# A two-block fp32 transformer kernel: the first product taken for both row tiles in turn, its loads in smaller pieces, the convolution ahead of one split

## The reference

```python
def causal_depthwise_conv3(u, w):
    s = u.shape[1]
    up = jnp.pad(u, ((0, 0), (CONV_W - 1, 0), (0, 0)))
    return up[:, 0:s] * w[0] + up[:, 1:s + 1] * w[1] + up[:, 2:s + 2] * w[2]

def short_conv_mixer(h, w_in, conv_w, w_out):
    bcx = h @ w_in
    b_gate, c_gate, u = jnp.split(bcx, 3, axis=-1)
    y = b_gate * causal_depthwise_conv3(c_gate * u, conv_w)
    return y @ w_out

mix = short_conv_mixer(rmsnorm(h, a_pre_norm[l]), a_w_in[l], a_conv_w[l], a_w_out[l])
h = h + rmsnorm(mix, a_post_norm[l])
```

## Time and profile before

| what | value |
| --- | --- |
| median of 3 runs | 1029.12 us (1028.97 to 1029.18) |
| the profiled execution | 1029.98 us |
| its span, first to last instruction | 1028.2 us |
| mean granted TensorE clock of the span | 0.998 |
| PE busy | 1020.1 us, 99% |
| DVE, ACT, POOL busy | 67%, 55%, 13% |
| data moved | 203.56 MB, mean 198 GB/s |

### The profile page before, as it was taken

The page is one execution under the profiler, slowest core; times in us unless marked ns, Lnnn a source line. Parts: engine busy times, 40 slices in busy tenths (PEclk is TensorE's granted clock), DMA queues, the critical chain, the costliest instruction groups (busy, mean ns, idle before and its releaser), DMA issues.

```text
span 1028.2 us, 14332 instructions
## 1 busy us (share of the span) xinstructions
PE 1020.1 (99%) x4783; PEld 839.0 (82%) x4783; DVE 684.2 (67%) x1034; ACT 567.0 (55%) x925; POOL 137.1 (13%) x219
## 2 busy tenths in 40 slices
PE   9999999999999999999999999999999999999997
PEld 6999888888877778888888888888887688888886
DVE  5777856656788985656668565656787685655643
ACT  5665654545567864444556454454676854454542
POOL 1100450000143152000014000000400220000002
PEclk9999999999999999999999999999999999999999
DMA  9575577566643467667576775757643355757551
GB/s 364 174 238 187 184 226 242 179 226 200 211 145 126 146 225 249 217 196 243 178 235 210 233 222 188 245 176 243 207 168 122 98 171 176 239 184 238 187 175 46
DMA packets 104174, 203.56 MB, mean 198 GB/s; under 512 B 52976, under 2 KB 57472, under 8 KB 104128
## 3 DMA queue, kind: packets, MB, share of 16 engines
q1 hardware_dynamic: 101952, 197.44, 59.0%
q0 software_dynamic: 1888, 5.17, 1.8%
q10 hardware_dynamic: 288, 0.37, 0.1%
HBM read 187.20 MB, written 1.05 MB: 183 GB/s over the span
## 4 chain that ended last, share of the span: by engine, by line
PE 96%; DVE 1%; ACT 1%; DMA 0%; POOL 0%; issue 0%; POOLq 0%; DVEq 0%; SPq 0%; ACTq 0%
PE pG L2108 16%; PE pG L2116 16%; PE pG L2112 16%; PE pD L2108 11%; PE pD L2112 11%; PE pD L2116 11%; PE pG L2097 2%; PE pG L2101 2%; PE pG L2098 2%; PE pT L2125 1%; PE pD L2142 1%; PE pD L2101 1%; PE pD L2097 1%; PE pD L2098 1%; PE pG L2422 1%; PE pG L2125 1%
## 5 line engine op out<-in xcount | busy, mean ns | idle before, releaser
L1693 DVE TENSOR_TENSOR w_low<-raw,w_high 128x1024 fp32r<-128x1024 f32 x340 | 410.3, 1225 | 195.8 <-ACT w_high L1370 185.7
L1370 ACT ACTIVATE w_high<-raw 128x1024 fp32r<-128x1024 f32 x340 | 354.7, 1056 | 207.0 <-PE pG L2116 135.9
L2108 PE MATMUL pG<-w_high,xTh 128*128 128x512 f32 x712 | 220.0, 390 | 0.0
L2112 PE MATMUL pG<-w_high,xTl 128*128 128x512 f32 x712 | 219.6, 389 | 0.0
L2116 PE MATMUL pG<-w_low,xTh 128*128 128x512 f32 x712 | 219.4, 390 | 0.2 <-DVE w_low L1693 0.2
L2116 PEld LDWEIGHTS pG<-w_low,xTh 128*128 128x128 f32 x712 | 133.6, 188 | 28.2 <-DVE w_low L1693 0.6
L2112 PEld LDWEIGHTS pG<-w_high,xTl 128*128 128x128 f32 x712 | 133.6, 188 | 28.1 <-DVE xTl L1739 0.2
L2108 PEld LDWEIGHTS pG<-w_high,xTh 128*128 128x128 f32 x712 | 133.3, 188 | 27.3
L1484 ACT ACTIVATE gate<-pG,stat 128x256 f32<-128x256 f32 x102 | 48.4, 474 | 140.1 <-PE pG L2116 124.0
L2108 PE MATMUL pD<-w_high,aTh 128*128 128x512 f32 x348 | 107.8, 391 | 0.0
L2116 PE MATMUL pD<-w_low,aTh 128*128 128x512 f32 x348 | 107.5, 390 | 0.0
(11 more groups left out here) (312 smaller groups left out, 1112.9 us busy)
## 6 DMA issues: line engine op xcount, KB each, us to landing
raw<-in_stream SPq DMA_DIRECT2D x340, 512.0 KB, 4.6
aF<-aB SPq DMA_DIRECT2D x320, 32.0 KB, 2.6
post<-in_posts POOLq DMA_DIRECT2D x5, 512.0 KB, 4.7
early<-in_stream SPq DMA_DIRECT2D x4, 512.0 KB, 13.1
xF<-hg SPq DMA_DIRECT2D x32, 64.0 KB, 2.5
xF<-hg POOLq DMA_DIRECT2D x32, 64.0 KB, 2.3
first_w<-in_stream SPq DMA_DIRECT2D x3, 512.0 KB, 5.8
h<-in_x SPq DMA_DIRECT2D x2, 512.0 KB, 11.9
```

Source lines behind the costliest of these rows:

```text
L1370: sc.activation(w_high[:, slot(static):slot(static) + CHUNK], raw_of(static), ACT.Copy).then_inc(w_high_done, 1)
L1693: ve.tensor_tensor(w_low[:, slot(static):slot(static) + CHUNK], raw_of(static), w_high[:, slot(static):slot(static) + CHUNK].bitcast(F32), ...
L2108: pe.matmul(dst, ah, w_high[:, where:where + n], start=start, stop=False)
L2112: pe.matmul(dst, al, w_high[:, where:where + n], start=False, stop=False)
```

## The change

`first` takes the two tiles in turn for each group of 128 features, so that each piece of `first_w` serves both at once. `first_w` is loaded in six pieces of 512 columns and the quarters and halves of `xt` go between them. DVE's `opening` makes four products of 256 columns and then two of 512, in place of `turn` for phase 0. ACT loads only the 91 columns of gains and taps; the identity follows on SP's queue behind `raw` 0, and PE waits for it behind `first`. Two of the 11 matmuls on zeros go. The turning of tile 0's block 0 moves one group later in block 1's product. ACT's `high` of chunks 3, 4 and 5 moves behind the next step of the convolution (or gate). Some semaphores are merged (`halo_and_logs`, `proj_done0`, `end_weights`), with waits for the same events.

```diff
-TURN_IN_PRODUCT = (2, 2)
+TURN_IN_PRODUCT = (3, 2)
-WARM_UPS = 11
+WARM_UPS = 9
+PIECE = 512
...
 def walk_first_block(step):
-    step("turn", 0, 0)
-    step("first", 0)
+    step("opening", 0)
     step("parts", 0, 0)
-    step("turn", 1, 0)
-    step("first", 1)
+    step("opening", 1)
+    step("first",)
     split(step, 0)
     step("norm", 0)
     split(step, 1)
     step("G", 0, 0, 0)
     split(step, 2)
-    step("high", 3)
     step("T", 0, 0, 0)
-    step("low", 3)
-    step("high", 4)
+    split(step, 3)
     step("Y", 0, 0, 0)
-    step("low", 4)
-    step("high", 5)
+    split(step, 4)
...
 def walk_second_block(step):
     step("G", 0, 1, 0)
-    step("low", 5)
+    split(step, 5)
     split(step, 6)
...
-                sp.dma_start(xt[0][:, 0:512], x_turned[0, :, 0:512]).then_inc(xt_left, 16)
+                left_quarter, second_quarter, right_half = slice(0, 256), slice(256, 512), slice(512, D)
+                load_x(0, left_quarter, xt_first)
                 first_weights(0)
+                load_x(1, left_quarter, xt1_loaded)
                 first_weights(1)
-                sp.dma_start(xt[0][:, 512:D], x_turned[0, :, 512:D]).then_inc(xt_right, 16)
+                load_x(0, second_quarter, xt_second)
+                load_x(1, second_quarter, xt_second)
                 first_weights(2)
-                sp.dma_start(xt[1][:], x_turned[1]).then_inc(xt1_loaded, 16)
+                load_x(0, right_half, xt_right)
+                load_x(1, right_half, xt_right)
+                for i in (3, 4, 5):
+                    first_weights(i)
                 load_raw(0)
+                sp.dma_start(consts[:, C_ID:C_FEATS], consts_in[:, C_ID:C_FEATS]).then_inc(ident_loaded, 16)
                 load_h(0)
...
-                sc.dma_start(consts[:, 0:C_ROPE], consts_in[:, 0:C_ROPE]).then_inc(ident_loaded, 16)
+                sc.dma_start(consts[:, C_FEATS:C_ROPE], consts_in[:, C_FEATS:C_ROPE]).then_inc(xt_first, 16)
...
+            def opening(half, ph):
+                if half == 0:
+                    ve.wait_ge(xt_first, 32)
+                    gained_quarter(0, 0).then_inc(warm_ready, 1)
+                    ve.wait_ge(xt1_loaded, 16)
+                    gained_quarter(1, 0).then_inc(warm_ready, 1)
+                    ve.wait_ge(xt_second, 32)
+                    for t in range(2):
+                        gained_quarter(t, 1).then_inc(hg_ready[t], 1)
+                else:
+                    ve.wait_ge(xt_right, 32)
+                    for t in range(2):
+                        gained(t, GAIN[0], 1, xt[t][:, 512:D])
...
+            def first(ph):
+
+                for kt in range(KT):
+                    for i in range((kt * MIX.cols + PIECE - 1) // PIECE, ((kt + 1) * MIX.cols - 1) // PIECE + 1):
+                        pe.wait_ge(first_loaded[i], 16)
+                    for t in range(2):
+                        if kt == 0:
+                            pe.wait_ge(warm_ready, t + 2)
+                        elif kt in (2, 4):
+                            pe.wait_ge(hg_ready[t], kt // 2)
+                        mm = pe.matmul(gate_bank(MIX, t, 0)[:, 0:MIX.cols], hg[t][:, kt * P:(kt + 1) * P],
+                                       first_w[:, kt * MIX.cols:(kt + 1) * MIX.cols], start=kt == 0, stop=kt == KT - 1)
+                        if kt == KT - 1:
+                            mm.then_inc(first_done1 if t else g_done0, 1)
                 pe.wait_ge(ident_loaded, 16)
```

More of the change, by code:

```diff
@@ L911, in build @@
         w_freed = sem("w_freed")
-        first_loaded = [sem(f"first_loaded{i}") for i in range(FIRST)]
+        first_loaded = [sem(f"first_loaded{i}") for i in range(FIRST * CHUNK // PIECE)]
         first_done1, warm_ready = sem("first_done1"), sem("warm_ready")
         h_loaded = rows2("h_loaded")
-        xt_left, xt_right, xt1_loaded = sem("xt_left"), sem("xt_right"), sem("xt1_loaded")
+        xt_first, xt_second, xt_right, xt1_loaded = sem("xt_first"), sem("xt_second"), sem("xt_right"), sem("xt1_loaded")
         ident_loaded, tables_loaded = sem("ident_loaded"), sem("tables_loaded")
@@ L1035, in moved_block, with x_count @@
             return network(ph) * (ph.nb - 1) + b + t + shift * (RING // (ph.cg + ph.kd))
+        def x_count(i):
+            return 3 + i + (1 if i < 3 else 2)
         def branch_done(eng, t, k, half):
@@ L1083, in first_weights, with load_x @@
                 def first_weights(i):
-                    sp.dma_start(first_w[:, i * CHUNK:(i + 1) * CHUNK], stream[i]).then_inc(first_loaded[i], 16)
+                    cols = slice(i * PIECE, (i + 1) * PIECE)
+                    sp.dma_start(first_w[:, cols], stream[i * PIECE // CHUNK][:, i * PIECE % CHUNK:i * PIECE % CHUNK + PIECE]).then_inc(first_loaded[i], 16)
+                def load_x(t, cols, loaded):
+                    sp.dma_start(xt[t][:, cols], x_turned[t, :, cols]).then_inc(loaded, 16)
                 def load_raw(c):
@@ L1337, in finish @@
                     pool.wait_ge(h_ready[0], 2 * FFN4.index + half + 1)
[L1338 removed]
+                    weighted(0, slice(512 * half, 512 * half + 512)).then_inc(end_weights, 1)
                 pool.wait_ge(end_m, 1)
[L1340 to L1342 removed]
+                pool.tensor_tensor(rr[0], ms[0], half_neg[:, 0:1], ALU.pow).then_inc(end_weights, 1)
+                pool.wait_ge(end_weights, 3)
                 pool.tensor_scalar(hg[0][:, 0:512], hg[0][:, 0:512], rr[0], None, ALU.mult).then_inc(out_by_pool, 1)
                 pool.wait_ge(end_m, 2)
[L1345 removed]
+                pool.tensor_tensor(rr[1], ms[1], half_neg[:, 0:1], ALU.pow).then_inc(end_weights, 1)
             steps = {f.__name__: f for f in (start, parts, squares, rest, norm, right, second_low, spread, reload, finish, tail, rope, S, LAT, VC, decay, GNvar)}
@@ L1711, in low, with gained_quarter @@
                 split_low(c, c)
+            def gained_quarter(t, quarter):
+                cols = slice(256 * quarter, 256 * quarter + 256)
+                g = feats[:, 2 * quarter:2 * quarter + 2].unsqueeze(2).broadcast_to([P, 2, P])
+                return ve.tensor_tensor(hg[t][:, cols].rearrange("p (k r) -> p k r", k=2), xt[t][:, cols].rearrange("p (k r) -> p k r", k=2),
+                                        g, ALU.mult)
             def gained(t, col, half, src):
@@ L1745, in turn @@
                     sinks()
-                if p == 0:
-                    for half in range(2):
-                        ve.wait_ge(xt1_loaded if t else (xt_left, xt_right)[half], 16)
-                        gained(t, GAIN[p], half, xt[t][:, 512 * half:512 * half + 512])
-                elif (t, p) not in RIGHT_ONLY:
+                if (t, p) not in RIGHT_ONLY:
                     for half in range(2):
                         gained_half(t, p, GAIN[p], half)
+            def opening(half, ph):
[11 more added lines that the diff above has]
+                        gained(t, GAIN[0], 1, xt[t][:, 512:D])
             def left(t, ph):
@@ L2084, in RL @@
                                  xTh[t][:, 4:8, :].rearrange("p k r -> p (k r)").bitcast(F32), ALU.subtract).then_inc(catT_ready[t], 1)
-            steps = dict(start=start, low=low, R=refill, left=left, turn=turn, parts=parts, second=second, second_low=second_low, spread=spread, gain=gain, rest=rest, finish=finish, tail=tail, join=join, G=G, V=V, T=T, Y=Y,
+            steps = dict(start=start, low=low, R=refill, opening=opening, left=left, turn=turn, parts=parts, second=second, second_low=second_low, spread=spread, gain=gain, rest=rest, finish=finish, tail=tail, join=join, G=G, V=V, T=T, Y=Y,
                          rope=rope, QKT=QKT, S=S, N=N, AT=AT, LAT=LAT, KPE=KPE, U=U, RROPE=RROPE, RSUM=RSUM, MT=MT, MS=MS, MN=MN, VC=VC, RT=RT, RM=RM, GNvar=GNvar, GNout=GNout,
@@ L2131, in start @@
                     pe.matmul(pD[1][:, 0:512], warm[:, 0:P], warm[:], start=True, stop=True)
-                pe.wait_ge(ident_loaded, 16)
-            def first(t, ph):
-                for kt in range(KT):
-                    if kt % 4 == 0:
-                        pe.wait_ge(hg_ready[t], kt // 4 + 1)
-                    if t == 0:
-                        for i in range((kt * MIX.cols + CHUNK - 1) // CHUNK, ((kt + 1) * MIX.cols - 1) // CHUNK + 1):
-                            pe.wait_ge(first_loaded[i], 16)
-                    mm = pe.matmul(gate_bank(MIX, t, 0)[:, 0:MIX.cols], hg[t][:, kt * P:(kt + 1) * P],
-                                   first_w[:, kt * MIX.cols:(kt + 1) * MIX.cols], start=kt == 0, stop=kt == KT - 1)
-                mm.then_inc(first_done1 if t else g_done0, 1)
+            def first(ph):
[11 more added lines that the diff above has]
+                            mm.then_inc(first_done1 if t else g_done0, 1)
+                pe.wait_ge(ident_loaded, 16)
             def turn(t, p, ph):
```

44 lines of the change are left out of this document (18 added, 26 removed).

## The result

| | before | after |
|---|---|---|
| median of the runs, us | 1029.07 (1028.93 to 1029.46, 12 runs) | 1031.4 (1030.86 to 1031.96, 12 runs) |
| ratio, 95% interval | | 1.0022 [1.0015, 1.003] |
| profiled execution, us (span) | 1029.98 (1028.2) | 1031.96 (1030.1) |

The change makes the kernel slower by 2.3 us; I had forecast no change, 1029.1, with 1028.3 to 1029.8 as the range. The profiled execution of before, 1029.98, lies above all twelve runs of its kernel, and 1031.96 is the highest of the twelve after. Keep this in mind wherever a time from one profile stands beside a median. The page of the profile says little: PE is busy for the same 1020.1 us as in the earlier trace rows, in a span that is 1.9 us longer.

A forecast was written before the change was run, and what follows sets the result against it. PE bounds the kernel (busy 1020.1 of 1028.2 us), ACT and DVE its opening's end. First product 0.5 us earlier, turning +0.52, ACT's order +0.07, loads 0: sum +0.1, 1030.1 profiled, median 1029.1; range 1028.3 to 1029.8.

The forecast's parts named there:

- What bounds the kernel: Opening: PE bounds up to 18.5 us, ACT and DVE up to 23.16; the gain is how much earlier that turning comes.
- The first product's start: `first` on PE: starts at 5.35 us, not before 5.20 nor after 6.32, since 0.45 MB less must land first.
- rivals 2: Opening: the whole start is gained, ACT and DVE not being the bound; 1.1 us, 1028.0, chance 0.05.
- 4: Start of `first`: small loads start no sooner, so it begins at 6.2 and the time is 1029.7; chance 0.11.
- The other pieces have room: Loads during `first`: second quarters land at 6.7, right halves at 8.6 us; needed at 8.8 and 11.4.
- DMA and SP: Loads up to `h`: 12 issued in place of 6, same bytes; priced at 0, bounds 0 and +0.3 us.
- The turning and ACT's order: Block 1's product to second turning: turning behind nine passes costs 0.52 us, ACT's later splits 0.07.
- The clock's rise (1): `first` on PE: clock already up when it begins, second turning about 22.45; 0.7 us less, 1028.4, chance 0.20.
- The slower case (3): `first` on PE: idle gap delays the clock's rise, 0.5 us per us; worst 1038.7; chance 0.06, half beyond 0.2%.
- 0.04 for slower: Whole kernel: chance given to a slower result, beside 0.94 same and 0.02 faster; about 0.2%, 2.1 us, can be told.

The follow-up runs named there:

- experiment 4: The changed kernel with the constants loaded as before (109.5 KB in one load, none for the identity): 1031.17 us, ratio 1.0018.
- experiment 5: The kernel before with two extra 512 KB loads ahead of `raw` 0, the squares waiting for them too: 1031.78 us, ratio 1.0025.
- 14: The kernel before with short constants, DVE's split of chunk 3 ahead of block 0's taps and 10 matmuls on zeros: 1029.44 us, ratio 1.0002.
- Experiment 6: The kernel before with only the changed order: turning behind nine passes, ACT's splits 3 to 5 behind the taps: 1030.03 us, ratio 1.0007.
- experiment 15: The kernel before once more, unchanged and profiled anew: 1029.23 us, ratio 1.0001.
- Experiment 8: The kernel before with 5 matmuls on zeros in place of 11: 1031.25 us, ratio 1.0019.
- experiments 1: The changed kernel with coarse loads again, `first_w` in three of 512 KB and `xt` in four of 256 KB: 1032.92 us, ratio 1.0027.
- 2: The kernel before with only the changed kernel's fine loads of `first_w` and `xt`, first product in the old order: 1033.98 us, ratio 1.0046.
- experiment 9: The changed kernel with coarse loads of `first_w` and `xt` and 15 matmuls on zeros in place of 9: 1030.81 us, ratio 1.0016.
- 11: The kernel before with `first_w` in six loads of 256 KB, in runs of 1024 bytes: 1031.03 us, ratio 1.0021.
- experiments 10: The kernel before with `first_w` in six loads of 256 KB, rows of 2048 bytes: 1029.61 us, ratio 1.0004.
- experiment 12: The kernel before with `first_w` in three loads of 512 KB, two of them with runs of 2048 bytes: 1031.4 us, ratio 1.0021.
- 13: The kernel before with `first_w` in four loads of 384 KB, in runs of 1024 bytes: 1035.92 us, ratio 1.0064.
- experiment 3: The kernel before with each load of `xt` and `first_w` cut in two by partitions, 64 rows each: 1033.44 us, ratio 1.0041.

## Why the prediction was wrong

**What bounds the kernel: right.** "What the change is worth is therefore how much earlier the turning at 23.16 comes", it says. In all 18 profiles the time of the profiled execution is its turning and 1006.5 to 1006.8 us, with turnings from 22.48 to 29.00, so the two go together within 0.4 us. What I missed is that 23.16 was the turning of an execution 0.9 us above its median. Against it the medians look off: order +0.2 in the turning and +0.7 in the median, late landings +1.9 and +2.5, and turnings of 22.5 to 22.8 that bring no gain. Against the 22.6 of a median execution, an estimate, they fit to 0.1 or 0.2 us.

**The first product's start: close, and worth nothing.** (So rivals 2 and 4, a gain of the whole start and no earlier start, are both out.) 5.35 forecast, 5.00 measured, below my lower bound of 5.20 (the record of the last matmul on zeros runs to 5.21 and overlaps it; I had taken an end for a start).

**"The other pieces have room": wrong.** At 410 GB/s I had the second quarters at 6.7 and the right halves at 8.6. At 243 GB/s the second quarters were there only at 7.6 and the right halves at 11.1, and the pieces of `first_w` came late too. PE waited for them inside the product, which ended at 17.71 in the prediction's way of counting, not at 16.75: the whole of the earlier start was given back, and 0.47 us more.

**DMA and SP: the step that failed.** The prediction says: "Even if the small pieces made the chunks land 0.5 late, the splits 1 and 2 [...] have 0.5 us of room against the taps [...]. I price it at 0 (bounds 0 and +0.3)." The chunks landed 2.4 late and `h` 2.6, five times the allowance. The room was mis-sized as well. In the four profiles whose chain goes through the squares of `h` (the change, experiments 4, 5 and 14) the turning comes 9.38 or 9.39 us behind their start. Before it came 9.88 behind, so 0.5 us of room was there in that one execution; with a turning at 22.6 (the estimate above) there is next to none. So in the medians nearly all of the delay shows: `h` 2.4 later gave 2.5 us in experiment 5, and 1.85 later gave 1.8 in experiment 4; in the change it's 2.3 for the 2.6 read in the highest of its runs. A term priced at 0 was worth the whole loss. The reasoning that broke was "the bytes up to `h` are the same": it carried the rate of the earlier trace rows, measured on loads of 256 and 512 KB, over to loads of 128 and 256 KB. That left the term without an honest bound. No row of before had twelve small loads in flight; what it had, 266 GB/s up to 6.20, I read as the time to get going only, and as a bound for a start-up that lasts 5 us longer it would have given about (413 - 266)/413 of 5 us, 1.8 us more. SP's own issues, 12 in place of 6, put the issue of `h` from 4.46 to 8.33; I priced the queue's order and not its time.

**The turning and ACT's order: right.** Experiment 6 gives 1.86 and 4.69 where I had 1.84 and 4.67. In the change itself the same order is behind later inputs. In the timeline it's 3.34 from the start of block 1's product to `cv`, where 1.78 before and 0.52 for three passes make 2.30; the other 1.04 is the wait for split 1. I had looked at the operands of the turning and not at those of the three passes put ahead of it. From `cv` to the turning it's 4.68. That the old order loses as much when `h` is late (experiment 5, by way of ACT) shows that this new dependence adds little.

**The rivals.** The clock's rise (1) didn't matter to the change, since the first product isn't on the chain; that it moves from run to run is seen in experiment 15, where the eleven matmuls on zeros take 4.24 us in place of 4.87. The slower case (3) had the right sign and the wrong mechanism. Experiment 8 shows its price, close to what I had: a rise 3 us later, behind a gap of 2.6 us, costs 1.55 us in the turning. I had no rival in which the loads get slower, and 0.04 for slower was far too little: with one term unmeasured on both sides, the slow side should have held more.

## What to carry to other kernels

When a load that PE waits for is cut into pieces, count what stands behind it in the queue: here the start came 1.3 us earlier and what stood behind the pieces 2.4 to 2.6 us later. A transfer rate read from large loads isn't a bound for small ones; ask for a row with loads of that size, and where there is none, price the slow side too. A profile is of one execution: see first where its time lies among the runs, since here a baseline that was 0.5 us late passed for room and hid that `h` was already due. And a wait of 2.4 to 3.2 us ahead of the first product cost the clock's lower level on top of itself in experiments 1, 2 and 8; matmuls on zeros up to the landing gave it back (2.1 us between the medians, in experiment 9).

## What the runs showed of the hardware

- Loads of HBM rows into 128 partitions, between 4 and 9 us: 413 GB/s with six loads, 359 with nine (2048-byte rows of `first_w`), 284 with nine (runs of 1024 bytes), 243 to 270 with twelve; about 410 again from 9 us on, when the queue holds large loads. The DMA share was 0.82 in the change, 0.90, 0.92 and 0.94 in experiments 4, 11 and 2, but 1.02 and more in experiments 10, 12 and 13, so a full share isn't a full rate.
- Loads into 64 partitions (experiment 3): 243 GB/s at a share of 0.99 from 4 to 9 us and 235 at 1.05 from 9 to 14, with rows of 4096 and 2048 bytes.
- SP's issues of loads took 0.40 to 0.43 us each for the first ten loads of the change, 0.51 for the eleventh, and 0.63 to 0.80 for the next four.
- The granted clock's column can say 1.00 where the pace of the matmuls is half (experiments 1 and 8); the count of matmuls in a stretch is the surer reading. A wait of 1.8 us inside the product, behind matmuls at the upper level, cost nothing of the clock in experiment 12 (28 records in 9.30 us).
- One program's first product started at 6.32 and at 6.01, and its turning at 23.16 and at 22.96, in two profiled executions of 1029.98 and 1029.56 us.
